# First compression round moved into the input projection, second round copied by GpSimd alone over nine units, output matrix loaded in halves

## The reference

```python
p = einsum('btd,dc->btc', rmsnorm(x, norm1_g), w_in)          # 1024 -> 1816 columns: q, three kv pairs, gates, pooling input
# keys and values in blocks of 64 positions, each block compressed by a product with a 64x64 matrix per position
kc = einsum('bnlkd,lde->bnke', blk[:, :, :, 0], w_cmp_k)
vc = einsum('bnlkd,lde->bnke', blk[:, :, :, 1], w_cmp_v)
o_cmp, p_kv = compressed_attention(q, q_pos, rmsnorm(kc), vc, slopes)
idx, valid = select_blocks(p_kv, q_pos, nb)                    # 16 best blocks
o_slc = selected attention over those blocks; o_win = attention over the last 512 positions
A = gate_merge(o_cmp, o_slc, o_win, gates); M = pool_mix(u)
h = x + concat(A, M) @ w_out
y = h + hier_moe(rmsnorm(h), ...)                              # 16 experts, each row uses two
```

## Time and profile before

| | us |
|---|---|
| median of 3 runs | 784.98 (784.39 to 786.95) |
| the profiled execution | 788.33, span 786.7 |
| PE busy | 730.6 (93%) |
| DVE busy | 267.7 (34%) |
| ACT busy | 172.1 (22%) |
| POOL busy | 186.0 (24%) |
| HBM traffic | 243 GB/s over the span |

### The profile page before, as it was taken

The page is one execution under the profiler, slowest core; times in us unless marked ns, Lnnn a source line. Parts: engine busy times, 40 slices in busy tenths (PEclk is TensorE's granted clock), DMA queues, the critical chain, the costliest instruction groups (busy, mean ns, idle before and its releaser), DMA issues.

```text
span 786.7 us, 16071 instructions
## 1 busy us (share of the span) xinstructions
PE 730.6 (93%) x6460; PEld 411.3 (52%) x6460; DVE 267.7 (34%) x695; ACT 172.1 (22%) x367; POOL 186.0 (24%) x313
## 2 busy tenths in 40 slices
PE   6999998899889787888879999999999999999998
PEld 3555546656566554566735545345555544455542
DVE  1200071355647557766402337311111000111147
ACT  3100031344656533423201101101110011011000
POOL 2000044467667562644100000100000000000050
PEclk9999999989999659999989999999999999999999
DMA  9856645301910892656896019488999999999964
GB/s 282 228 163 210 202 105 116 121 2 56 318 58 17 260 338 65 174 155 186 231 408 271 27 55 357 166 319 318 402 407 419 428 414 424 420 420 419 393 251 144
DMA packets 74479, 191.76 MB, mean 244 GB/s; under 512 B 13718, under 2 KB 48806, under 8 KB 69917
## 3 DMA queue, kind: packets, MB, share of 16 engines
q1 hardware_dynamic: 62565, 154.82, 54.7%
q0 software_dynamic: 9600, 27.77, 10.4%
q10 hardware_dynamic: 2240, 8.13, 2.6%
HBM read 174.09 MB, written 16.70 MB: 243 GB/s over the span
## 4 chain that ended last, share of the span: by engine, by line
PE 77%; DVE 9%; issue 5%; DMA 5%; POOL 1%; ACT 1%; POOLq 1%; SPq 1%; DVEq 0%; ACTq 0%
PE bank L1319 30%; PE bank L879 13%; PE bank L1220 7%; PE bank L923 4%; PE bank L1027 2%; PE bank L876 2%; DMA arena<-in_w_out 2%; PE bank L1303 2%; DVE arena L1946 1%; PE bank L1166 1%; PE bank L1071 1%; PE bank L1040 1%; PE bank L1411 1%; PE bank L1211 1%; PE bank L1240 1%
## 5 line engine op out<-in xcount | busy, mean ns | idle before, releaser
L1319 PE MATMUL bank<-arena,proj 128*32 128x256 f32 (+1 forms) x2352 | 238.7, 483 | 1.3 <-DVE proj L2164 0.8
L1319 PEld LDWEIGHTS bank<-arena,proj 128*32 128x32 f32 x2352 | 103.6, 110 | 96.1 <-issue 77.7
L879 PE MATMUL bank<-arena,amT 128*128 128x454 f32 x256 | 101.1, 553 | 0.8 <-DVE amT L1661 0.8
L2352 POOL DMA_INDIRECT proj<-normed_rows,idx x12 | 11.4, 954 | 309.1 <-PE bank L1303 192.4
L2174 DVE TENSOR_TENSOR proj<-proj,bank 128x256 f32<-128x256 f32 x24 | 10.0, 422 | 209.8 <-PE bank L1319 209.8
L879 PEld LDWEIGHTS bank<-arena,amT 128*128 128x128 f32 x256 | 48.6, 193 | 49.2 <-issue 48.0
L1220 PE MATMUL bank<-arena,amT 128*128 128x512 f32 x128 | 57.8, 608 | 6.6 <-DMA arena<-in_w_out 6.6
L2291 POOL DMA_DIRECT2D arena<-in_cache_slc_kv x96 | 51.5, 536 | 52.5 <-issue 46.0
L1319 PE MATMUL bank<-amT,proj 128*32 128x512 f32 (+1 forms) x336 | 56.5, 532 | 0.0
L1319 PE MATMUL bank<-queries_and_bias,proj 128*32 128x512 f32 (+1 forms) x384 | 56.5, 486 | 0.0
L1220 PEld LDWEIGHTS bank<-arena,amT 128*128 128x128 f32 x128 | 24.5, 196 | 35.5 <-issue 28.7
(11 more groups left out here) (374 smaller groups left out, 1135.7 us busy)
## 6 DMA issues: line engine op xcount, KB each, us to landing
arena<-in_w_up SPq DMA_DIRECT2D x13, 2048.0 KB, 16.7
arena<-in_w_down SPq DMA_DIRECT2D x13, 2048.0 KB, 16.3
arena<-in_w_gate SPq DMA_DIRECT2D x10, 2048.0 KB, 17.1
arena<-in_cache_cmp_kv SPq DMA_DIRECT2D x96, 128.0 KB, 2.2
amT<-in_w_gate SPq DMA_DIRECT2D x3, 2048.0 KB, 14.5
queries_and_bias<-in_w_gate SPq DMA_DIRECT2D x3, 2048.0 KB, 11.7
expert_rows<-proj ACTq DMA_DIRECT2D x11, 512.0 KB, 9.7
arena<-in_w_in SPq DMA_DIRECT2D x3, 1816.0 KB, 7.5
```

Source lines behind the costliest of these rows:

```text
L879: last = pe.matmul(ps(("in", c, i))[0:n, 0:WC], xnT[:, k, i * P:i * P + n], w_in[c % 2][:, k, :], start=k == 0, stop=k == KC - 1)
L1319: ins = pe.matmul(dst[part, :], rows[:, part], own if q < TRIO else shared, start=start, stop=stop)
```

## The change

Round 0 moves ahead: its 64 steps stand in nine row tiles of the input projection, from tile 1 of column block 2 to the last tile of block 3, at two places of each tile. Its matrices come in four quarters of 16 steps through two buffers in `xh`. Pages of sequences 0 and 1 are loaded by SP, those of 2 and 3 by GpSimd, as soon as the second projected tile is done. GpSimd copies the 64 chunks of round 0 before it norms the keys. The squares of q go tile by tile through two 512-column buffers, because their old place is taken. The bank plan leaves banks 4 and 5 to the compression up to the attention.

Pages of sequences 4 and 5 are loaded by SP in two parts around the end of the projection, those of 6 and 7 by GpSimd after the key norm. Round 1 stands in units 5 to 13, about seven steps in each, and GpSimd makes all 64 copies; VectorE and ScalarE make none. The chain of the compressed branch moves from units 21 to 29 to units 15 to 21. `raw(0)` stands ahead of VectorE's copies of the turned keys.

Rows 512 to 1023 of the output matrix go to two places that are free once the prompt attention is over (the bias area, and columns of `proj` already stored), issued by SP in the sample attention; the first half stays where it was. The slot that is free for it takes one expert matrix ahead of the output projection. The gain row of the second norm is waited for together with x.

```diff
-CMP_UNITS = [(0, 6), (15, 5)]
+CMP_UNITS = [(0, 0), (5, 9)]
 RING = 8
-BEFORE = 3
+EARLY_GROUPS = 9
+QUARTER = 16
+IN_BANKS = (0, 1, 2, 3, 6, 7)
...
-    idle = [(0, i, s) for i, s in enumerate((2, 3, 4, 5, 0, 1, 6, 7))]
+    idle = [(0, i, s) for i, s in enumerate((2, 3, 4, 5, 1, 0, 6, 7))]
...
-def compress_before(i):
-
-    return [(0, d) for d in range(BEFORE * i, BEFORE * (i + 1))]
+def compress_within(c, i):
+
+    k = (c - 2) * TILES + i - (2 * TILES - EARLY_GROUPS)
+    return share([(0, d) for d in range(HD)], EARLY_GROUPS, k) if k >= 0 else []
...
-    for r, (first, count) in enumerate(CMP_UNITS):
-        if first <= u < first + count:
-            done = BEFORE * TILES if r == 0 else 0
-            return share([(r, d) for d in range(done, HD)], count, u - first)
-    return []
+    first, count = CMP_UNITS[1]
+    return share([(1, d) for d in range(HD)], count, u - first) if first <= u < first + count else []
...
-    21, 22, 25, 26, 28, 29, 23, 29
+    15, 16, 18, 19, 20, 21, 17, 21
...
+
+    def add(name, bank=None):
         if bank is None:
-            bank = nxt[0] % pool
...
-        qn = [view(xflat, 4096 + i * 512, 512) for i in range(2)]
...
+            [qflat[:, TILES * 256 + 4 * SLOTS * i:TILES * 256 + 4 * SLOTS * (i + 1)] for i in range(2)], [row4[:, 0:4 * SLOTS], row4[:, CU:CU + 4 * SLOTS]])]
...
         SLC = 2 * 4096
...
+        qn = [shares[:, :, :].rearrange("p a b -> p (a b)"), second[:, :, :].rearrange("p a b -> p (a b)")]
...
 
-        w_out = view(arena, SLC, KC, D)
+        w_out = view(arena, SLC, 4, D)
...
+            def load_later(b):
+
+                sp.load(regs, table_rows[b:b + 1, :])
...
+                    sp.dma_start(cache[:, (b - 4) * PAGES + k, :], src).then_inc(ld_cache, 16)
...
+                for kv, w in enumerate((a["w_cmp_k"], a["w_cmp_v"])):
+                    for par in range(2):
+                        sp.dma_start(w_quarter[q % 2][64 * par:64 * par + 64, kv, :, :], w[:, q * QUARTER:(q + 1) * QUARTER, :])\
+                            .then_inc(ld_quarter[q % 2], 16)
...
-            load_cache(0, 0, 2)
+            for par in range(2):
+                sp.dma_start(posr[64 * par:64 * par + 64, :], a["cmp_pos_emb"]).then_inc(ld_pos, 16)
+            load_cache(0, 2)
+            sp.wait_ge(act_sq, TILES)
+            filled(sp, ("xT", TILES - 1, 1))
+            load_quarter(0)
             filled(sp, ("in", 0, TILES - 1))
             load_win(2)
-            load_cache(0, 2, 2)
+            load_quarter(1)
             filled(sp, ("in", 1, TILES - 1))
             load_win(3)
-            sp.wait_ge(heads_ms, 1)
-            load_wcmp(1)
-            for par in range(2):
-                sp.dma_start(posr[64 * par:64 * par + 64, :], a["cmp_pos_emb"]).then_inc(ld_pos, 16)
+            for q in (2, 3):
+                sp.wait_ge(chunk_used, QUARTER * (q - 1))
+                load_quarter(q)
+            sp.wait_ge(regrouped, regrouped_at(0, HD - 1))
+            load_later(4)
             filled(sp, ("in", 3, TILES - 1))
             sp.dma_start(sel[0:NS, :, :], a["c_sel"]).then_inc(ld_sel, 16)
...
-            load_wcmp(0)
...
+            load_later(5)
+            for par in range(2):
+                filled(sp, ("cmp", 0, par))
+            load_wcmp(1)
+            load_wcmp(0)
...
-            sp.wait_ge(regrouped, regrouped_at(0, HD - 1))
-            for b in (4, 5):
-                sp.load(regs, table_rows[b:b + 1, :])
...
-            sp.wait_ge(regrouped, regrouped_at(1, HD - 2))
-            sp.wait_ge(by_vector, HD // 4)
-            sp.wait_ge(by_scalar, HD // 4)
+            sp.wait_ge(regrouped, regrouped_at(1, HD - 1))
...
+                if t == 2:
+
+                    for k in range(KVH):
+                        filled(sp, ("p_T", NP - 1, k))
+                    filled(sp, ("p_o", NW - 1))
+                    sp.wait_ge(st_out, 16 * N_OUT)
+                    sp.dma_start(w_out_late, a["w_out"][512:768, :].rearrange("(k p) c -> p k c", p=P)).then_inc(ld_wout, 16)
+                    for k in range(2):
+                        src = a["w_out"][768 + P * k:768 + P * (k + 1), :].rearrange("p (h c) -> p h c", h=2)
+                        sp.dma_start(w_out_rows[:, 2 * k:2 * k + 2, :], src).then_inc(ld_wout, 16)
...
-            sp.dma_start(w_out[:, 4:8, :], a["w_out"][512:1024, :].rearrange("(k p) c -> p k c", p=P)).then_inc(ld_wout, 16)
...
-            sp.dma_start(g2b, spread(a["norm2_g"].rearrange("(a n) -> a n", a=1), 0, P)).then_inc(ld_g2, 16)
+            sp.dma_start(g2b, spread(a["norm2_g"].rearrange("(a n) -> a n", a=1), 0, P)).then_inc(ld_xr, 16)
...
-                if n == 4:
+                if n == 5:
                     filled(sp, ("h", TILES - 1, 1))
...
+            def compress(r, d):
+
+                if d == 0:
+                    for par in range(2):
+                        opened(pe, ("cmp", r, par))
+                    if r == 1:
+                        pe.wait_ge(ld_wcmp, 64)
+                if r == 0 and d % QUARTER == 0:
+                    pe.wait_ge(ld_quarter[d // QUARTER % 2], 64 * (d // QUARTER // 2 + 1))
+                pe.wait_ge(regrouped, regrouped_at(r, d))
+                n = 2 * slots_of(r)
+                for par in range(2):
+                    rows = slice(64 * par, 64 * par + 64)
+                    for kv in range(2):
...
+                        if c >= 2 and k % 4 == 2:
+                            for r, d in share(compress_within(c, i), 2, k // 4):
+                                compress(r, d)
...
-                for r, d in compress_before(i):
-                    compress(r, d)
...
-            pe.wait_ge(ld_wout, 16 * 9)
+            pe.wait_ge(ld_wout, 16 * 11)
...
-                    sc.activation(qsq, proj[:, :, 0:512], ACT.Square).then_inc(heads_sq, 1)
...
-                    sc.wait_ge(heads_ms, 1)
+                    for i in range(TILES):
+                        if i >= 2:
+                            sc.wait_ge(heads_ms, i - 1)
+                        sc.activation(qn[i % 2], proj[:, i, 0:512], ACT.Square).then_inc(heads_sq, 1)
+                    sc.wait_ge(heads_ms, TILES + 1)
...
-                for r, d in compress_steps(u + 1):
-                    if r == 1 and d % 4 == 3:
-                        sc.wait_ge(regrouped, regrouped_at(0, HD - 1) + 1)
-                        chunk_free(sc, r, d)
-                        sc.activation(chunk_out(r, d), chunk_in(r, d), ACT.Copy).then_inc(by_scalar, 1)
...
+            raw(0)
...
-                for r, (first, count) in enumerate(CMP_UNITS):
-                    if u == first + count:
-
-                        raw(r)
-                        for par in range(2):
-                            taken(ve, ("cmp", r, par))
-                        if r == 1:
-                            ve.tensor_tensor(ktmp, kcr, kcr, ALU.mult).then_inc(kc_sq, 1)
+                if u == sum(CMP_UNITS[1]):
+
+                    raw(1)
+                    for par in range(2):
+                        taken(ve, ("cmp", 1, par))
+                    ve.tensor_tensor(ktmp, kcr, kcr, ALU.mult).then_inc(kc_sq, 1)
...
-                for r, d in compress_steps(u + 1):
-                    if r == 1 and d % 4 == 1:
-                        ve.wait_ge(regrouped, regrouped_at(0, HD - 1) + 1)
-                        chunk_free(ve, r, d)
-                        ve.tensor_copy(chunk_out(r, d), chunk_in(r, d)).then_inc(by_vector, 1)
...
-            ve.wait_ge(ld_xr, 16 * TILES)
+            ve.wait_ge(ld_xr, 16 * (TILES + 1))
...
+                po.load(page_regs, a["page_table"][b:b + 1, :])
...
+                    po.dma_start(cache[:, b % 4 * PAGES + k, :], src).then_inc(ld_last, 16)
...
+            def regroup(r, d):
+
+                chunk_free(po, r, d)
+                po.tensor_copy(chunk_out(r, d), chunk_in(r, d)).then_inc(regrouped, 1)
+
+            filled(po, ("in", 0, 1))
+            cmp_pages(2)
+            cmp_pages(3)
+            po.wait_ge(ld_pos, 32)
+            alone(po.tensor_copy(cache[:, 64, :].rearrange("p (a d) -> p a d", d=HD),
+                                 spread(posr.rearrange("p (a d) -> p a d", a=1), 1, 4)), regrouped)
+            po.wait_ge(ld_cache, 32 * 16)
+            po.wait_ge(ld_last, 32 * 16)
+            filled(po, ("xT", TILES - 1, 1))
+            po.wait_ge(act_sq, TILES)
+            for d in range(HD):
+                regroup(0, d)
+
             po.wait_ge(heads_rt, 2)
...
-            for i in range(TILES):
-                filled(po, ("in", 3, i))
-            po.wait_ge(ld_pos, 32)
-            alone(po.tensor_copy(cache[:, 64, :].rearrange("p (a d) -> p a d", d=HD),
-                                 spread(posr.rearrange("p (a d) -> p a d", a=1), 1, 4)), regrouped)
+            po.wait_ge(regrouped, regrouped_at(0, HD - 1))
+            cmp_pages(6)
+            cmp_pages(7)
...
-            po.wait_ge(ld_cache, 64 * 16)
-            po.wait_ge(q_ready, 1)
```

(9 more changed lines are left out.)

132 lines of the change are left out of this document (61 added, 71 removed).

## The result

The change made the kernel slower. The median is 798.1 us (797.8 to 798.5, 4 runs) against 786.0 us of the kernel before on the same chip (784.4 to 787.9, 4 runs), a ratio of 1.0154 with a 95% interval of 1.0127 to 1.0181. The forecast was 757, with a range of 747 to 773. The profiled execution took 797.8 us, its span 796.2.

The account below looks back on a forecast made before the run. The prediction took TensorE as the bound (77% of the chain that ended last), with slack between 151.7 and 300. Prompt attention ending 21.5 us earlier and 6.6 at the output matrix made -28.1, from 784.98 to 757 us, range 747 to 773.

Parts of the forecast that it names:

- Round 0 in the projection: Input projection: 64 steps at 0.22 us and 18 switches at 0.16 add 17.2 us, none hidden; bounds 14.1 to 17.7.
- The third block of w_in: Input projection: its load, behind six more DMAs on SP's queue, arrives about when wanted; cost 0, bounds 0 and 3.5 us.
- The switching cost: Entering and leaving the small tiles of a group of steps: 0.16 us each, 2.9 us for 18 half groups in the projection.
- the rival of a falling clock: Small tiles drop the granted clock in the projection from 77 to 143.5, making the kernel slower, 823 us; chance 0.07.
- Round 1's start: Attention, unit 5: TensorE, GpSimd's pages and the matrices all meet at 189 to 190, where before it was 223.9.
- the one in which both supplies fail: Rival: the pages of both rounds come late together, +24 to +26 us, 782 or 783, no change; chance 0.04.
- the starved round 0: Rival: the projection stands still until round 0's pages are in, +15 us, 772; chance 0.08.
- GpSimd's pace: Rival: GpSimd's 64 copies pace round 1, 49 to 58 us from 182, to 240; +9 us, 766; chance 0.14.
- Round 1 itself: Attention, units 5 to 13: steps and switches 19.3 us, units 23, together 42 us, ending at 231.5 instead of 251.7.
- The tail: Round 1's end to prompt attention's end: 48 us, +13.2 for six units, -14.5 for clock and waits, 46.8; bounds 292 to 271.5.
- The rival of a tail set by latency: The compressed branch's chain through several engines sets the tail whatever surrounds it; 10 us less gained, 767; chance 0.22.
- The output matrix: Output projection: loading 2 MB during the sample attention removes TensorE's wait, -6.6 us; other bound -0.7.

Follow-up runs that it names:

- e1: Changed kernel with the third block of the input matrix issued before the first quarter of the compression matrices instead of after it: ratio 1.0066 to the kernel before.
- e4: Changed kernel with the round 0 steps of each projection tile at one place, after its fourth product, instead of two: ratio 1.0076 to the kernel before.
- e3b: Changed kernel with seven eighths of round 1's key compression matrix loaded in the projection, the rest and the value matrix right behind the selection table: ratio 0.9997.
- e5: Changed kernel with the compressed branch's chain back at its old places, units 21 to 29 instead of 15 to 21: ratio 1.0174 to the kernel before.
- e8: Changed kernel with each of the sixteen 16-column products of the compressed branch's chain issued twice: ratio 1.018 to the kernel before, tail 63.4 us.
- e7: Kernel before with only the output matrix loaded in halves, one by unit 31, the other after the selected branch: ratio 0.9897 to the kernel before.
- e2: Changed kernel with the fifteen stores of new keys and values issued after round 1's last copy: ratio 1.0128 to the kernel before.
- e13: Changed kernel with third input block earlier, most of key matrix in projection, one step place per tile, distances before value matrix, gates as scalar operands: ratio 0.9876.

## Why the prediction was wrong

**Round 0 in the projection**, forecast +17.2, measured +27.3. Three terms. The third block of w_in was taken at 0 with a bound of 3.5, by the six small issues ahead of it; block 2 began 5.0 later (0.7 of it also in e1), because I counted what its issue is queued behind on SyncE and not the 1 MB that its bytes are queued behind: it landed 13.97 us after its issue. e1 shows it. The lower clock behind that standstill adds 1.8. The switching cost was read from groups that stand between transposes, where the earlier trace rows give 0.16; among the 454-column products it is 0.37 (e4), and by this the 18 places cost 3.8 more than forecast and the 64 steps (0.213 each) 0.7 less, 3.1 together. The three terms make 9.9 of the 10.1. The rest of this step was right: 0.22 a step, no wait for GpSimd's copies, and the granted clock at 1.00, so the rival of a falling clock was rightly held unlikely. The transposes (-4.3) and the key norm (10.1 us, covered) came as forecast.

**Round 1's start**, forecast 189 to 190, measured 214.3. TensorE's arrival (199.1) was right but for the 10 us of the projection, and so was the last issue of the matrices (189.7, forecast 179.5). GpSimd's register load began 10 us late for the same reason (158.0, forecast 148), and its issues took longer: 32.4 us to the last one, where before they took 27.8 (188.6 to 216.4). The last row of each, before, then after:

```profile
212.21 4.21 POOL L2283 DMA_DIRECT2D arena<-in_cache_cmp_kv  x7 [0.38 <-issue]
...
185.52 4.85 POOL L2283 DMA_DIRECT2D arena<-in_cache_cmp_kv  x8 [5.11 <-issue]
```

That is some 4.5 us more, whose cause isn't shown. The step that failed is the landing: from the last issue to the copy it took 22.0 us instead of 4.4. I took GpSimd's 32.2 us of before, from register load to last landing, as if they belonged to GpSimd. In the kernel before, the pages had the queues for themselves, since the matrices were loaded in and right after the projection. The change issues 4 MB of matrices (186.7 to 189.7) beside GpSimd's last eight pages (185.5 to 190.4), and each was priced by a row in which the other was absent. The pages landed up to 22.4 us after issue.

The matrices failed by a second error. The 9.9 us of the earlier trace rows are those of loads issued two at a time, 2 MB, and from 107.7 to 117.7 in the kernel before, with nothing beside them but two small loads, the queues moved 205 GB/s. At that rate the 4 MB that are now issued at once need some 20 us (an estimate), so they could not have been in at 189 even with the queues for themselves. They took up to 25.0. So an earlier landing of the pages alone would have left TensorE waiting. e3b gets 12 us back by moving 1.8 MB into the projection and the rest ahead of the pages. No rival had this step: the one in which both supplies fail adds the starved round 0 (+15) and GpSimd's pace (+9), and neither came about. Of the signs of being wrong, the wait on a GpSimd copy showed it (15.22 us).

**Round 1 itself**, forecast 42, measured 43.3, with GpSimd alone at 0.60 us a copy instead of 0.76: right. The rival of GpSimd's pace falls.

**The tail**, forecast 46.8, measured 60.7. Its first term is near: the six added units were priced at 13.2 and by e5 take 16.1 (260.2 to 276.3). The other, -14.5 for clock and waits among wider units, is what failed, and all of it: e5 shows that the chain costs 18 us among the wide units, 16 of them TensorE's busy time. Its own thin products are 10.6 us at the lower clock (3.62 + 6.99), and e8 shows the 6.99 on the path. Cover can't hide work of the engine that is the bound. What the clock can give is seen in e4, whose tail is 4.1 us shorter with the same instructions. The bound of the forecast, nothing recovered (292), would have been the right value for this step: 48 + 13.2 = 61. The rival of a tail set by latency (767) had the sign and most of the size (10 us of 14) and not the reason: the chain costs about the same wherever it stands, but by TensorE's work and not by the other engines.

**The output matrix**, forecast -6.6, measured -7.5 in the changed kernel (92.0 us from the first sample keys to the output projection, 99.5 before) and -6.3 in e7: right.

So the sum of what was gained and lost against before is: projection and transposes +22.9 at the first scores, -34 forecast and -8.8 measured at the start of round 1, +18.7 at the sample keys, +11.2 at the output projection. The range failed because it was taken from single rivals, while three errors of one sign came together (10.1, 14.9 and 14.2 us), the second of them on a step that had no bound. The first two are of one kind: what else the queues carry was left out. That the kernel would be slower had 0.07, for a falling clock in the projection, which didn't come.

What stays open: the moment at which the clock falls in the tail. Kernels with the same TensorE instructions there had tails of 56.6 (e2) to 63.2 us (e13). The stretch of 0.50 lay on the thin products in the changed kernel and behind them in e13 (280 to 300), but no run here fixed that moment.
